# Output projection and p-gate by seven block products, with held-back last products

## The reference

```python
for i in range(DEPTH):                       # DEPTH = 2
    a = rms_norm(h, attn_norm[i])
    proj = a @ w_in[i]
    y_da, y_ssd, y_gla = ...                  # attention, SSD, GLA: 512 columns each
    mix = jnp.concatenate([y_da, y_ssd, y_gla], axis=-1)
    h = h + mix @ w_out[i]                   # 256x1536 @ 1536x1024: the projection
    f = rms_norm(h, ffn_norm[i])
    h = h + (silu(f @ w_ffn_gate[i]) * (f @ w_ffn_up[i])) @ w_ffn_down[i]
    h = h + sigmoid(h @ ple_w_gate[i]) * (p[i] @ ple_w_proj[i])   # 256x1024 @ 1024x1024: the gate
```

## Time and profile before

| | |
|---|---|
| median of 3 runs | 1683.04 us (1682.68 to 1684.2) |
| the profiled execution | 1682.88 us, of which the span of instructions 1681.2 us |
| TensorE matmuls busy | 1643.7 us, 98% of the span |
| VectorE busy | 799.1 us, 48% |
| ScalarE, GpSimd busy | 183.1 us, 57.3 us |
| projection, layer one and two | from 178.85 and 627.14 us |
| gate, layer one and two | from 437.10 and 886.18 us |

### The profile page before, as it was taken

One profiled execution on the slowest core, in us unless ns is written; L12 is line 12 of the kernel. 1 busy time (PEld: TensorE's weight loads), 2 busy tenths in 40 slices (PEclk: granted clock), 3 DMA queues, 4 the chain that ended last, 5 costly groups with the idle time before them and its releaser, 6 DMA issues.

```text
span 1681.2 us, 19180 instructions
## 1 busy us (share of the span) xinstructions
PE 1643.7 (98%) x8200; PEld 1048.1 (62%) x8200; DVE 799.1 (48%) x1401; ACT 183.1 (11%) x287; POOL 57.3 (3%) x85
## 2 busy tenths in 40 slices
PE   6999999999999999999999999999899999999996
PEld 3775489974458654999545867887544444444442
DVE  3787276764259852766642666701521222212122
ACT  1321000000104110000001420500100000000000
POOL 2000030000010010000000000000000000000000
PEclk9999999999999999999999999999899999999999
DMA  5542365453443324564535323444899999999994
GB/s 156 196 144 75 134 189 180 151 180 120 175 157 121 121 100 134 180 194 155 190 107 200 116 85 109 167 150 160 340 413 427 426 428 428 426 428 428 427 428 163
DMA packets 116334, 374.49 MB, mean 223 GB/s; under 512 B 9796, under 2 KB 57416, under 8 KB 104216
## 3 DMA queue, kind: packets, MB, share of 16 engines
q1 hardware_dynamic: 112736, 370.36, 57.8%
q0 software_dynamic: 1136, 2.17, 0.6%
q10 hardware_dynamic: 2376, 0.72, 0.2%
HBM read 372.18 MB, written 1.05 MB: 222 GB/s over the span
## 4 chain that ended last, share of the span: by engine, by line
PE 95%; DMA 2%; DVE 1%; ACT 1%; issue 0%; ACTq 0%; POOLq 0%; POOL 0%; SPq 0%; DVEq 0%
PE bank L900 16%; PE bank L1216 12%; PE bank L677 10%; PE bank L625 10%; PE bank L951 8%; PE bank L1259 6%; PE bank L636 6%; PE bank L1085 5%; PE bank L1193 3%; PE bank L1226 3%; PE bank L1025 2%; DMA arena<-in_w_up 2%; PE bank L1015 2%; PE bank L1136 2%; PE bank L644 1%; PE bank L991 1%
## 5 line engine op out<-in xcount | busy, mean ns | idle before, releaser
L1216 PE MATMUL bank<-arena,mix 128*64 128x512 f32 x640 | 167.8, 592 | 2.1 <-DMA arena<-in_w_up 1.9
L625 PE MATMUL bank<-weights,xT 128*128 128x512 f32 x384 | 168.9, 597 | 0.8 <-DVE xT L1556 0.8
L677 PE MATMUL bank<-weights,xT 128*128 128x512 f32 x320 | 139.1, 593 | 2.6 <-ACT arena L1294 2.6
L625 PEld LDWEIGHTS bank<-weights,xT 128*128 128x128 f32 x384 | 72.7, 192 | 88.0 <-issue 86.7
L1216 PEld LDWEIGHTS bank<-arena,mix 128*64 128x64 f32 x640 | 55.0, 137 | 110.4 <-issue 110.4
L900 PE MATMUL bank<-arena 128*128 128x128 f32 x1056 | 121.5, 275 | 0.0
L900 PEld LDWEIGHTS bank<-arena 128*128 128x128 f32 x1056 | 119.7, 192 | 0.0
L2477 DVE TENSOR_TENSOR mix<-mix,bank 128x512 f32<-128x512 f32 x16 | 16.9, 1057 | 207.4 <-PE bank L1216 207.4
L1216 PE MATMUL bank<-weights,mix 128*64 128x512 f32 x384 | 111.9, 592 | 0.0
L677 PEld LDWEIGHTS bank<-weights,xT 128*128 128x128 f32 x320 | 60.0, 190 | 75.9 <-issue 75.9
L636 PE MATMUL bank<-xT,weights 128*128 128x256 f32 x448 | 98.5, 380 | 0.0
(11 more groups left out here) (431 smaller groups left out, 2044.6 us busy)
## 6 DMA issues: line engine op xcount, KB each, us to landing
weights<-in_w_in SPq DMA_DIRECT2D x30, 2048.0 KB, 8.2
arena<-in_w_gate SPq DMA_DIRECT2D x20, 2048.0 KB, 17.3
arena<-in_w_up SPq DMA_DIRECT2D x20, 2048.0 KB, 21.0
arena<-in_w_down SPq DMA_DIRECT2D x20, 2048.0 KB, 22.8
weights<-in_w_gate SPq DMA_DIRECT2D x12, 2048.0 KB, 19.2
weights<-in_w_up SPq DMA_DIRECT2D x12, 2048.0 KB, 20.2
weights<-in_w_ffn_gate SPq DMA_DIRECT2D x22, 1024.0 KB, 5.4
weights<-in_w_ffn_up SPq DMA_DIRECT2D x22, 1024.0 KB, 8.0
```

Source lines behind the costliest of these rows:

```text
L625: ins = mm(b[:, :], xT[:, k, t0 + P * t:t0 + P * t + P], w[:, k, :], start=(k == 0), stop=(k == KD - 1))
L677: ins = mm(banks[i][:, :], lhs(k, t), w[:, k % 4, 512 * half:512 * half + 512], start=(k == 0), stop=(k == last))
L1216: ins = mm(moe_bank[bank][SL * e:SL * e + SL, :], xsE[:, k, SL * e:SL * e + SL], w[e][:, k, :], start=(k == 0), stop=(k == KD - 1), skip_g ...
```

## The change

Both products become sums over chunks of a 2x2 block product (token halves by column halves, the rows of a chunk in two interleaved halves) by seven products. The projection has three such chunks (DA, SSD, GLA part), the gate two. Each product is two matmuls of 128x512 a chunk and accumulates over the chunks in its own bank. VectorE makes the operand sums (`row_sums`, taken out of `down_sums`), reads out and combines (`Seven`), and for the gate writes the pre-activation to `sg`; ScalarE's sigmoid then runs in place on `sg`.

Order on TensorE: p2, p1, p6, p5, p3 give the first token half and a quarter of the second; p7 and p4, which only the second half needs, of the last chunk and of the chunk ahead of it come at the end, and the turn of the normed first half stands behind them. `out_chunk_sums(0)` stands on VectorE ahead of the GLA gating, `out_chunk_sums(1)` and `(2)` ahead of `gate_up_sums(0)`. `out_chunk_sums(2)` waits until chunk 0's p4 is done. The tile lists grow (`wo` and `pg` from 4 to 7).

```diff
-    ("z", 2), ("daT", 2), ("gg", 2), ("ssdT", 2), ("wo", 4), ("glaT", 2),
-    ("n2", 4), ("ffn", 2 * KF), ("pT", 1), ("dn", 7), ("pp", 4), ("n3", 4), ("pg", 4),
+    ("z", 2), ("daT", 2), ("gg", 2), ("ssdT", 2), ("glaT", 2), ("wo", 7),
+    ("n2", 4), ("ffn", 2 * KF), ("pT", 1), ("dn", 7), ("pp", 4), ("n3", 4), ("pg", 7),
...
+            def seven(tile, name, a, a_sum, w, w_sum, first, last):
+                lhs, rhs = dict(p1=(a(0, 0), w(0, 0)), p2=(a(0, 1), w(1, 0)), p3=(a_sum(3), w(1, 1)), p4=(a(1, 1), w_sum(3)),
+                                p5=(a_sum(0), w_sum(0)), p6=(a_sum(1), w_sum(1)), p7=(a_sum(2), w_sum(2)))[name]
+                k = tile + SEVEN[name]
+                b = claim(k) if first else psum[k % NPS]
+                pairs = w(0, 0).shape[1]
+                for j in range(pairs):
+                    ins = mm(b[:, :], lhs[:, j, :], rhs[:, j, :], start=(first and j == 0), stop=(last and j == pairs - 1))
+                return ins.then_inc(psum_full(k), 1) if last else ins
...
-                ch = rows_out(T("wo"), ch, KM, lambda k, t: xcols((k + 8) % KM, t), 4, lambda: turn(T("n2"), xn, 0, "xn_ready"),
-                              ahead={4: gla_turn, 8: lambda: mix_turned("glaT")})
+                out(0, "p2", "p1")
+                mix_turned("ssdT")
+                pe.wait_ge(chunk_full(ch + 1), full_at[ch + 1])
+                out(1, "p2", "p1")
+                pe.wait_ge(sem("out_sums"), n.next("out_sums"))
+                out(0, "p6", "p5", "p3", "p7")
+                mix_turn("glaT", "gla_mix_ready", 1024)
+                pe.wait_ge(sem("out_sums"), n.next("out_sums"))
+                out(1, "p6")
+                out(0, "p4").then_inc(sem("chunks_used"), 1)
+                out(1, "p5", "p3")
+                mix_turned("glaT")
+                pe.wait_ge(chunk_full(ch + 2), full_at[ch + 2])
+                out(2, "p2", "p1")
+                pe.wait_ge(sem("out_sums"), n.next("out_sums"))
+                out(2, "p6", "p5", "p3")
+                out(1, "p7", "p4").then_inc(sem("chunks_used"), 1)
+                out(2, "p7", "p4")
+                ch += 3
+                turn(T("n2"), xn, 0, "xn_ready")
...
+                for c in range(2):
+                    pe.wait_ge(chunk_full(ch + c), full_at[ch + c])
+                    gate(c, "p2", "p1")
+                for c in range(2):
+                    pe.wait_ge(sem("gate_sums"), n.next("gate_sums"))
+                    gate(c, "p6", "p5", "p3")
+                gate(0, "p7", "p4").then_inc(sem("chunks_used"), 1)
+                gate(1, "p7", "p4")
+                ch += 2
                 after = TILE["n1", layer + 1] if layer + 1 < DEPTH else TILE["m1"]
-                ch = rows_out(T("pg"), ch, KD, xcols, KD, lambda: turn(after, xn, 0, "xn_ready"))
+                turn(after, xn, 0, "xn_ready")
...
+                def first_half(self, h00, h01, h11):
+                    self.sum_of(h00, h00, "p2")
+                    self.p1_copied()
+                    self.plus(h00, h00, p1d)
+                    self.sum_of(self.u2, p1d, "p6")
+                    self.sum_of(self.u4, self.u2, "p5")
+                    self.plus(h01, h01, self.u4)
+                    self.plus(h11, h11, self.u4)
+                    self.sum_of(h01, h01, "p3")
+                def second_half(self, h10, h11):
+                    self.plus(self.u3, self.u2, self.landed("p7"))
+                    self.sum_of(h11, h11, "p7")
+                    self.plus(h10, h10, self.u3)
+                def last(self, h10):
+                    self.sum_of(h10, h10, "p4")
...
+                def out_chunk_sums(j):
+                    ch = layer * LAYER_CHUNKS + OUT_AT + j
+                    for t in range(NT):
+                        k = T(("daT", "ssdT", "glaT")[j]) + t
+                        v.wait_ge(psum_free(k), fills(k))
+                    v.wait_ge(chunk_full(ch), full_at[ch])
+                    if j == 2:
+                        v.wait_ge(sem("chunks_used"), freed[ch - 2][1])
+                    row_sums(x_blocks(MIX_AT[j]), lambda s_: hsum[:, j % 2, s_], down_blocks(ch, 2), out_sums(j), "out_sums")
...
+                out_chunk_sums(1)
+                out_chunk_sums(2)
                 gate_up_sums(0)
-                for t in range(NT):
-                    add_rows(T("wo"), t)
-                    sum_squares(t)
-                    scaled(t)
-                    norm_evac(T("n2"), t, cpl[:, 8:16])
+                part = Seven(T("wo"), [ud[:, i, :] for i in range(3)])
+                part.first_half(h_part(0, 0), h_part(0, 1), h_part(1, 1))
+                sum_squares(0)
+                scaled(0)
+                part.second_half(h_part(1, 0), h_part(1, 1))
+                norm_evac(T("n2"), 0, cpl[:, 8:16])
+                part.last(h_part(1, 0))
+                sum_squares(1)
+                scaled(1)
+                norm_evac(T("n2"), 1, cpl[:, 8:16])
```

More of the change, by code:

```diff
@@ L149, in first_loads @@
     cols(COL["gg"], 512, T("gg") + 1)
-    rows(out, d["w_out"][layer], KM, T("wo") + 3)
+    rows(out, d["w_out"][layer], KM, T("wo") + 6)
     g = d["w_ffn_gate"][layer].rearrange("(k p) n -> p k n", p=P)
@@ L157, in first_loads @@
     rows(out, d["ple_w_proj"][layer], 2, T("pp") + 3)
-    rows(out, d["ple_w_gate"][layer], KD, T("pg") + 3)
+    rows(out, d["ple_w_gate"][layer], KD, T("pg") + 6)
     return out
@@ L942, in down @@
                     pairs = 2 if j < DOWN_CHUNKS - 1 else KF // 2 - 2 * j
[L943 to L952, removed]
+                    return seven(T("dn"), name, hid_blocks(2 * j, pairs), lambda s_: hsum[:, j % 2, s_], down_blocks(ch + j, pairs),
+                                 lambda s_: wsum[:, (FFN_CHUNKS + j) % 2, s_, 0:512 * pairs].rearrange("p (a n) -> p a n", a=pairs), first, last)
                 DOWN_ORDER = ("p2", "p1", "p6", "p5", "p3", "p7", "p4")
@@ L1565, in add_rows, with step @@
                     v.wait_ge(psum_free(k), fills(k))
-            def gated_rows(layer, t):
-                for half in range(2):
-                    k = TILE["pg", layer] + 2 * t + half
-                    o = 512 * half
-                    v.wait_ge(psum_free(k), fills(k))
-                    s_ = sg[:, t, o:o + 512]
-                    TT(s_, s_, ppv[:, t, o:o + 512], ALU.mult).then_inc(sem("dve_step"), 1)
-                    v.wait_ge(sem("dve_step"), n.next("dve_step"))
-                    TT(h[:, t, o:o + 512], h[:, t, o:o + 512], s_, ALU.add).then_inc(sem("dve_step"), 1)
-                    v.wait_ge(sem("dve_step"), n.next("dve_step"))
-                if t == NT - 1:
+            def step():
+                v.wait_ge(sem("dve_step"), n.next("dve_step"))
@@ L2137, in _ @@
-                TT(u3, u2, p7, ALU.add).then_inc(sem("dve_step"), 1)
-                step()
-                added(1, 1, "p7")
-                added_sum(1, 0, u3)
-                landed("p4")
-                added(1, 0, "p4")
-                v.sem_inc(sem("h_ready"), 1)
+                part = Seven(T("dn"), [ud[:, i, :] for i in range(3)])
+                part.first_half(h_part(0, 0), h_part(0, 1), h_part(1, 1))
+                v.sem_inc(sem("h_ready"), 1)
+                part.second_half(h_part(1, 0), h_part(1, 1))
@@ new lines, in _ @@
+                part.last(h_part(1, 0))
+                v.sem_inc(sem("h_ready"), 1)
+                for t in range(NT):
+                    for half in range(2):
+                        k = T("n3") + 2 * t + half
+                        v.wait_ge(psum_free(k), fills(k))
+                for c in range(2):
+                    ch = layer * LAYER_CHUNKS + GATE_AT + c
+                    v.wait_ge(chunk_full(ch), full_at[ch])
+                    row_sums(x_blocks(4 * c), lambda s_: hsum[:, c, s_], down_blocks(ch, 2), gate_sums(c), "gate_sums")
```

142 lines of the change are left out of this document (91 added, 51 removed).

## The result

The changed kernel took 1687.96 us (median of 7 runs, 1685.24 to 1690.3), the kernel before 1683.1 (7 runs, 1681.18 to 1684.59). The ratio is 1.0027, with a 95% interval of 1.0015 to 1.0038: slower by 4.9 us, where 1679.8 was forecast and 1686.5 was the upper end of the range. The profiled execution took 1686.78 us around a span of 1685.0.

The account below looks back on a forecast made before the run. TensorE's own instruction stream was taken as the bound in both layers. Of 19.8 us gross, 0.2 (projections), 1.0 and 2.1 (gates) were to remain, 3.3 in all: 1679.7, stated as 1679.8 us, range 1675.0 to 1686.5.

Parts of the forecast that it names:

- the joints: Places in both layers where TensorE waits for VectorE's sums, adds and norm; laid out with start times, net gain 3.3 us.
- The FFN chunk's sums: VectorE's operand sums for the first FFN chunk, ahead of the first residual add: start forecast at 205.3, before 201.01.
- The first gate: Gate product of layer one: gain of 1.0 us forecast, with TensorE waits of 1.2 and 1.85 us.
- Four banks at once: End of layer two: the next stage claims four banks, the last holding p4; TensorE was to idle 3.4 us.
- three long joints: Both projections and the end of layer two, where waits were to eat most of the gain; forecast's chance 0.42.
- 19.8 us: Gross gain forecast: 20 fewer matmuls, 17.2 us, plus 2.6 us for the gate's wait for four banks, twice.
- the sparse stretches: Three new thin stretches on TensorE: 6.1 us with 0.87 of transposes per projection, 4.3 with 0.87 ending layer two.
- the clock as the rival: Clock falls in the new gaps, chance 0.32: 1685 at 1.8 us a gap, 1695 at 5.1; decides from 6.7 us.
- The 1.8: Lowest price in us of one clock fall in a new sparse stretch, from 8.86 against 7.03 us for 16 records.
- The row of 16 records at the start: 128x512 matmul records at the kernel's start: 8.86 us against 7.03 later, put down to the lower clock level.
- the second gate: Gate product of layer two: landing 0.45 us earlier, next stage starting at 913.45 against 915.54, gain 2.1 us.
- the cover holds better: First add not held by FFN chunk's sums, or slot back earlier: up to 5 us a projection, 1670 to 1675; chance 0.12.

## Why the prediction was wrong

**Right: the joints.** Of the times laid out for TensorE, those after the start-up shift of 1.00 us held to a few tenths. The FFN chunk's sums started at 206.80, forecast 205.3 + 1.0. The issue was at 198.09, where the slot was to be free at 196.89 + 1.0. The first residual add was the next thing in line, as said. The projection cost 0.11 us where -0.1 was forecast: waits of 2.73 and 1.45 us, where 2.65 and 2.6 stood, the second shortened because the transposes themselves had slowed down by 0.9 (in the projection-only kernel, with transposes at the full clock, it is 2.32). The first gate gained 1.36 us, forecast 1.0, with waits of 0.99 and 1.66 (1.2 and 1.85). Four banks at once made a gap of 3.19 us at the end of layer two (3.4).

**The step that failed: "The forecast (three long joints eat 16.5 of 19.8 us, clock up) has 0.42".** The prediction had the sparse stretches, named the clock as the rival, gave 1.8 to 5.1 us for each and 6.7 us in all as the point from which it decides, and then chose the clock that stays up, with "no gap here alone exceeds 3.4 us" against the rival. The trace of before held no gap of 2 to 3 us between matmuls ahead of the routing stage, so it couldn't bear that choice out: its only comparable stretch had a fall. The term that the sum put at nothing, the clock, measured 2.93, 1.45 and 1.40 us in the three stretches, 5.8 in all. (In each projection 0.9 more went into slowed transposes, and the second gap hid it.) Filling the gaps gives back 9.4 us by the medians (1687.96 to 1678.59), of which the rows give these 5.8 to the clock. In all the price is inside the rival's bounds (5.4 to 15.3), near their lower end, and two of the three stretches cost less than the 1.8 that was the least. It is also less than the 6.7 named as the point from which the clock decides: with it alone the sum is +2.5, and the rest is the smaller miss below. The rival's own time of 1685 was nearer than the forecast's.

The Trainium skill's page "TensorE: Matmul & The Clock Gate" (Part 1) says that the default of the gate is the throttled state and that only recent activity keeps it open. The trace agrees: the granted clock fell inside the gap of 2.73 us and stood at 0.50 through the eight transposes and the gap of 1.45 us behind them.

The 1.8 rested on a reading that the record doesn't bear out. The row of 16 records at the start was put down to the lower level, but the windows of the kernel before read a granted clock of 1.00 from 8 to 26 us. The eight transposes ahead of that row take 1.91 us, nearly twice the usual 1.04, so its slowness may still be the lower level. It isn't shown.

**A smaller miss: the second gate.** I took the landing of its second chunk to be earlier in layer two, and 2.1 us to be gained. The chunk landed 1.23 us late for TensorE, as the waits on ple_w_gate show, and 0.77 us were gained. Its transfer took 13.5 us from issue to landing, where it took 12.1 before. It took 12.3 with the gate alone and 12.2 with all gaps filled (waits of 0.32 and 0.22 us), but 13.5 with either gap filled alone, where no projection had a fall, and 13.5 to 13.9 in the four kernels with moved sums or single claims. So it isn't the clock that makes it late. What does is open.

**What the sum would have been.** With the clock up -3.3 us were forecast, and the filled kernel shows -4.5. With 5.8 us for the clock and 1.3 for the second gate (2.1 - 0.77) the sum is +3.8, the difference of the spans (+4.9 by the medians). That it fits so closely is partly chance: the start (+1.00) and the routing stage (-1.45) nearly cancel.

**Where the rest of the 19.8 us was.** The rival "the cover holds better" had named the order on VectorE as what stands against up to 5 us a projection. The moved sums show that: the FFN starts 4.2 us earlier in layer one, and the time is 1677.26 us. With the banks claimed one by one 1675.45, with the sums split 1671.07.

## What to carry to other kernels

When a change thins out a saturated engine, lay out the idle gaps that it makes as well as the work that it takes, and price each sparse stretch on TensorE at the lower clock as the likely case: here the kernels with two gaps of 1.5 to 3 us and eight transposes between them had a lower mean clock in all 28 runs, and in the profiled executions a fall cost the matmuls behind it 1.4 to 3.0 us. The gain comes from the chain that ends last at the joint. Operand sums that are needed later belong behind the norm that TensorE waits for, and a bank is claimed when it is filled. Filler matmuls are a quick test for whether the clock is what costs: 13 of them in the whole kernel, two or three to a gap, went with 9.4 us less. Check the joints before all of that is put down to the clock: the rows give it 5.8.

## What the hardware showed that I had not expected

- The lower clock can set in within a gap of 2.7 to 3.2 us and outlasts it: granted 0.75 at 218 to 220 us, 0.50 to 228, with matmuls back to back from 223.09. It can also set in behind the gap: in the gate-only kernel the windows read 1.00 to 912.0, with matmuls back to back from 911.58, and 0.50 from 912.5.
- The same gap doesn't always do it. 3.00 us ahead of the transposes passed at 1.00 in one profiled execution, 2.73 us didn't in another; the runs of the kernels with one gap left in each projection (and the one at the end of layer two) spread over 7.7 and 10.6 us, those of the kernel with all filled over 2.8.
- No gap of up to 1.7 us between dense stretches had a fall in any trace ahead of the routing stage.
- With 13 matmuls whose results nobody reads, the changed kernel was 9.4 us shorter.
- The routing stage, which no edit here touches, has a fall of 6.8 to 13.7 us in the profiled executions, so it moves times by itself: 1.5 us between the two kernels' profiled executions.
